# Attention on one core: VectorE takes each pair's copy before the next pair's maximum

## The reference, cut to what matters

```
def sink_attend(qb, keys, values, masks, sinks):
    scale = HEAD_DIM ** -0.5
    parts = []
    for kk, m in zip(keys, masks):
        s = jnp.einsum('bqhgd,bkhd->bhgqk', qb, kk).astype(jnp.float32) * scale
        if m is not None:
            s = jnp.where(m, s, -jnp.inf)
        parts.append(s)
    ...
    p = jax.nn.softmax(jnp.concatenate(parts + [sink], axis=-1), axis=-1).astype(qb.dtype)
    ...
```

## Time and profile before

| What | Value |
|---|---|
| Median of 3 runs | 2835.79 us (2835.55 to 2839.4) |
| The profiled execution's own time | 2838.26 us |
| Its span, first to last instruction | 2836.5 us |
| PE, DVE, ACT busy, share of the span | 94%, 66%, 51% |
| The attention stage | from 255 to 529 us in the span |
| DVE in the whole kernel | 3373 instructions, 1864.5 us busy |

### The profile page before, as it was taken

How to read it: one execution, slowest core, us unless ns; L and a number is a source line. 1 busy time by engine, 2 the same in 40 slices (tenths; PEclk the granted TensorE clock), 3 DMA queues, 4 the chain that set the end, 5 groups by cost and what they waited for, 6 DMA issues and landing times. The chain is left out here.

```text
span 2836.5 us, 40437 instructions
## 1 busy us (share of the span) xinstructions
PE 2669.5 (94%) x13974; PEld 1208.1 (43%) x13975; DVE 1864.5 (66%) x3373; ACT 1432.4 (51%) x3340; POOL 504.4 (18%) x404
## 2 busy tenths in 40 slices
PE   7998999899899999999999598997999999999994
PEld 2444666444333443434434264443333334333332
DVE  4996555576677666666665555765666667666655
ACT  1113555343176666666665241332656666666653
POOL 0000000111022222222222121100222222222212
PEclk9999999999999999999999799998999999999997
DMA  9777300201499999999999622016999999998996
GB/s 363 261 269 208 140 16 9 81 30 45 192 342 342 328 311 347 352 349 345 371 330 321 211 101 88 30 49 250 321 310 347 309 375 342 347 376 283 330 331 200
DMA packets 147094, 705.64 MB, mean 249 GB/s; under 512 B 18987, under 2 KB 24363, under 8 KB 94665
## 3 DMA queue, kind: packets, MB, share of 16 engines
q1 hardware_dynamic: 104252, 556.14, 50.3%
q0 software_dynamic: 42336, 144.81, 20.6%
q10 hardware_dynamic: 304, 2.11, 0.2%
HBM read 597.50 MB, written 114.84 MB: 251 GB/s over the span
## 5 line engine op out<-in xcount | busy, mean ns | idle before, releaser
L1693 ACT ACTIVATE xT<-xt_blocks 32x256 f32<-32x256 f32 x2208 | 916.3, 415 | 42.6 <-DVE xt_blocks L1560 15.1
L1772 PE MATMUL exG<-ring,xT 128*32 128x512 f32 (+2 forms) x2352 | 699.5, 597 | 2.9 <-DMA ring<-in_exp_w_up_dram 2.9
L1772 PEld LDWEIGHTS exG<-ring,xT 128*32 128x32 f32 (+2 forms) x2352 | 231.3, 140 | 308.5 <-issue 304.7
L1806 PE MATMUL exD<-ring,ex_hT 128*32 128x512 f32 (+2 forms) x1176 | 355.7, 605 | 2.4 <-DVE w_o L1598 1.2
L1565 DVE TENSOR_SCALAR ex_e<-ex_e 128x256 f32<-128x256 f32 x142 | 42.6, 300 | 426.7 <-ACT ex_e L1705 403.1
L1566 DVE RECIPROCAL ex_e<-ex_e 128x256 f32<-128x256 f32 x142 | 248.9, 1753 | 4.9
L1705 ACT ACTIVATE ex_e<-exG 128x256 f32<-128x256 f32 x142 | 54.6, 385 | 314.9 <-PE exG L1772 314.9
L1772 PE MATMUL exG<-oT,xT 128*32 128x512 f32 (+2 forms) x592 | 197.5, 599 | 1.3 <-DVE xT L1554 1.3
L1772 PE MATMUL exG<-w_fnet,xT 128*32 128x512 f32 (+2 forms) x608 | 176.8, 600 | 4.0 <-issue 4.0
L1524 DVE TENSOR_TENSOR mod<-place,slots 128x1024 bf16<-128x1024 f32 (+3 forms) x196 | 174.1, 912 | 4.5 <-PEq L234 3.6
L1806 PEld LDWEIGHTS exD<-ring,ex_hT 128*32 128x32 f32 (+2 forms) x1176 | 115.9, 141 | 129.1 <-issue 128.2
(11 more groups left out here) (424 smaller groups left out, 4314.9 us busy)
## 6 DMA issues: line engine op xcount, KB each, us to landing
ring<-in_exp_w_gate_dram SPq DMA_DIRECT2D x64, 1024.0 KB
ring<-in_exp_w_up_dram SPq DMA_DIRECT2D x64, 1024.0 KB
ring<-in_exp_w_down_dram SPq DMA_DIRECT2D x64, 1024.0 KB
ada_w<-in_w_ada_dram SPq DMA_DIRECT2D x48, 512.0 KB, 5.5
oT<-in_exp_w_gate_dram SPq DMA_DIRECT2D x17, 1024.0 KB
oT<-in_exp_w_up_dram SPq DMA_DIRECT2D x17, 1024.0 KB
oT<-in_exp_w_down_dram SPq DMA_DIRECT2D x17, 1024.0 KB
fT<-in_exp_w_gate_dram SPq DMA_DIRECT2D x17, 1024.0 KB
```

The costliest lines, as they stand in the source:

```text
L1693: last = act.activation(xT[m * UNIT:(m + 1) * UNIT, par, :, a * UNIT:(a + 1) * UNIT], parts[a * UNIT:(a + 1) * UNIT, m], ACT.Copy)
L1772: last = pe.matmul(psG[par][p:p + m], xT[:, par, k, p:p + m], ring[s % RING][:, 0:2, k * FF:(k + 1) * FF], start=k == 0, stop=k == KT - 1)
L1806: last = pe.matmul(psD[p:p + m, c], hT[:, k * P + p:k * P + p + m], ring[s % RING][:, 2, k * D + c * 512:k * D + (c + 1) * 512], start=k = ...
```

## The change

On VectorE, iteration p now does copy(p), then top(p + 1), then the bookkeeping. Only top(0) stands ahead of the loop. The number and kind of instructions are the same on every engine, and the order on PE, ACT, POOL and SP is as before.

```diff
                         top(0)
-                        top(1)
                         for p in range(N + 2):
                             if p < N:
                                 copy(p)
+                            if p + 1 < N:
+                                top(p + 1)
                             if p % 4 == 2 and p < N:
                                 sinks(p // 4)
                             if p % 4 == 3 and p < N:
                                 denominators(p // 4)
                             if p >= 5 and p % 4 == 1:
                                 divide(p // 4 - 1)
-                            if p + 2 < N:
-                                top(p + 2)
```

## The result

The changed kernel took 2839.51 us, median of 12 runs (2836.52 to 2843.02), against 2835.29 us before (median of 12). The ratio is 1.0017, 95% interval 1.0009 to 1.0025: +4.2 us by the medians, slower by less than the 0.2% set as the bound. The forecast was 2840.1. The profiled execution's own time was 2843.02 us, its span 2841.1.

What follows compares the result with a forecast made beforehand. PE bounds two iterations in four, a loop through DVE the other two. Middle rounds +1.3, edge rounds +2.0, start +0.4 and end +0.55 sum to +4.3 us: 2835.79 becomes 2840.1, range 2836.5 to 2844.5.

Steps and rivals of the forecast that it cites:

- The bound and the possible gain: Middle rounds: PE bounds two iterations in four; in the others DVE costs 0.41 us each, 0.8 us a round.
- the loop through DVE: Before the change: scores, maximum, bias, copy, scores, a loop through PE and DVE of 4.23 us in middle rounds.
- The new loop: Turn, copy, then the next pair's maximum, bias, exponentials and turn: 4.00 us in a middle tile, 3.57 in an edge tile.
- The second head takes the gain back: PE's fifth turn waits for the second head's exponentials, ready 0.78 us after the first; middle round +0.11 us.
- The sinks: Sinks step now behind the maximum it needs: 0.30 us on top of the loop for one pair in four.
- The sum: Attention stage: twelve middle rounds +1.3, four edge rounds +2.0, start +0.4, end +0.55, together +4.3 us.
- The rival of the held maximum: On DVE, the maximum is held until the copy is done: loop 0.08 us longer, +7.3 us in all, 2843.1; chance 0.17.
- the page's rule: On DVE, the next instruction waits until the pipe empties; the prediction instead took a start 0.08 us before the copy's end.
- The rival of a gain: PE's fifth turn does not wait for the second head: middle round 16.94 us, kernel 2831.1, -0.16%; chance 0.07.
- of nothing: Loop 0.1 us shorter than the rows say, or the ends cancel: within 1 us of before; chance 0.08.

Runs made afterwards that it cites:

- The orders in odd and in even iterations: Copy before the next maximum in odd or in even iterations alone, the kernel before's order elsewhere: stage 277.55 us (odd), 276.46 us (even).
- the repetition: The changed kernel, unaltered, timed again beside the kernel before: ratio 1.0011, median 2838.00 us against 2834.82, stage 278.25 us.
- The version with the copy in between: Against the kernel before, the copy placed between the next pair's maximum and its bias: ratio 0.9982, timed again 0.9976.

## Why the prediction was right

- **The bound and the possible gain.** Right. The early copy took 0.23 off each of the two iterations that the loop through DVE had bounded, and the scores no longer waited for it.
- **The new loop.** Each of its five steps was measured within 0.02 us of its term, and the loop at 4.00. Every term had a row before, the copy behind a waiting turn among them.
- **The second head takes the gain back.** This was the step that decided, and before it could be read only at the stage's ends. The changed trace shows it (0.36 at the fifth turn, in every second middle pair), and the experiment that delayed that head alone shows that it is on the path: 0.19 later, 0.37 a round longer. The orders in odd and in even iterations show where: only behind a short iteration does the wait cost time.
- **The sinks.** Hidden in the middle, 0.3 at the last pair, 0.03 in a full edge round: as reckoned.
- **The sum.** The middle rounds were reckoned at 17.52 and measured at 17.52. The start and the last pair came out as reckoned too: in the repetition the first two turns were 3.58 us apart (3.14 before, +0.44 for the 0.4 reckoned) and the last two 3.88 (3.32 before, +0.56 for 0.55). The edge tiles were overpriced. The sum has twelve middle rounds and four full edge rounds of +0.49. Counted by turns there are eleven middle ones and only two full edge rounds, which lost 0.53 each; the two that cross between an edge and a middle tile lost 0.29 (16.48 to 16.77) and 0.33 (15.76 to 16.09). From the first turn to the next stage the repetition took 4.0 us longer than before (273.90 against 269.92), not 4.3.
- **Where luck helped.** The medians differed by 4.2 us in the first timing and by 3.2 in the second, with intervals of 2.6 to 7.1 and 0.6 to 5.7. They can't confirm a forecast of 4.3 to the tenth; the rounds and the waits do that for the mechanism.
- **The rival of the held maximum, and the page's rule.** By the sentence in the Trainium skill's page "VectorE: DVE Perf Modes", section "The DRAIN you can't avoid", that the next instruction waits until the pipe is empty, the sum would have been 2843.1. The maximum started 0.60 or 0.61 behind the copy in every iteration read, not 0.69. The trace does not agree with that sentence by itself; it does agree with what the section adds, that a next instruction which is not held starts earlier.
- **The rival of a gain, and of nothing.** Rounds would have been 16.94, or about 17.4 for nothing. They were 17.52.

## What to carry to other kernels

When a step is moved off one loop between engines, write down the loop that it closes and add it up to the *last* thing that the next stage waits for, here the second head and not the first. A gain in one iteration that makes the next one stop is no gain: sum over the whole period, not over an iteration. An instruction that must wait for the result just ahead of it on its own engine leaves a gap (here 0.11 us between the maximum and its bias), and that is the place for independent work. Put there, the copy started 0.19 us earlier, which in two iterations of each round bought 0.4 us a round without moving the chain behind it onto the path.

## What the runs showed that was not expected

The stage starts after an idle stretch of PE of 2.8 us at the change of stage, and its first scores run at the lower of the two clock levels, 1.2 GHz (granted clock 0.50 from 257 to 258 us in all eleven traces). How long that lasts differs from one execution to the next. The same two windows, first in the trace before, then in the changed kernel's first trace (PEclk is the third figure from the end):

```profile
255.00:260.00 5.00, 4.50 (x23) 2.65 (x24) 2.09 (x5) 1.11 (x3) 0.11 (x1) 0.66 0.77 168
260.00:265.00 5.00, 3.26 (x26) 2.17 (x24) 3.34 (x6) 3.27 (x9) 0.00 (x0) 1.00 1.03 197
```

```profile
255.00:260.00 5.00, 3.87 (x18) 2.49 (x18) 1.90 (x4) 0.00 (x0) 0.52 (x1) 0.54 0.56 128
260.00:265.00 5.00, 3.98 (x25) 2.46 (x21) 2.05 (x4) 2.90 (x8) 0.00 (x0) 0.77 1.05 202
```

In the second the turns of the first pair, from 260.93, ran at the low level as well (0.50 from 260 to 262). The first turn came 4.80 us after the first scores instead of 4.48, and the second pair's turn 4.04 later where the repetition of the same kernel had 3.58: 0.8 us. The version with the copy in between had 4.80 and 3.79 in one trace, 4.19 and 3.15 in the other. The granted clock from 259 to 260 us sorts the traces: it was 0.50 in four (the changed kernel's first, the odd and the even iterations, the first with the copy in between), and in these the first turn came 4.80 or 4.81 us after the first scores; in the other seven it was 0.78 to 1.00, and the first turn came after 3.69 to 4.73. So the same kernel's stage differs by about 1 us between executions, most of it from this, and a stage time can't settle less than that; the rounds in the middle of the stage can. That is how the result of the even iterations has to be read.
